# Low parts of every fourth weight chunk made on GpSimd instead of VectorE

## The chip, the cores and the metric

The kernel runs on one core of one Trainium2 chip. The metric is the device time of one execution in microseconds. TensorE (PE) multiplies, VectorE (DVE) and ScalarE (ACT) work elementwise, SyncE (SP) issues the loads of the weights, and GpSimd (POOL) does nothing after four constants at the start.

## The reference, cut to what matters

Two blocks run one after the other on 256 tokens of 2048 features. The first has a retention layer (8 heads) and a sliding-window attention layer (16 query heads, 4 key and value heads); both have an adaptive norm before them. The second has three parallel branches (block attention, dilated attention, attention over a memory) that gates merge. In skeleton:

```
h   = rms_norm(x) * (1 + scale) + shift        # scale, shift: cond @ ada_w
p   = h @ w_in                                 # queries, keys, values, gates
y   = mixer(p) * silu(gate)
x   = x + gt * (y @ w_out)                     # twice, then the second block
```

Everything is float32, and nearly all the time goes into `h @ w`, with weights of some 490 MB that pass through the core once. To reach float32 accuracy with faster products, each weight matrix and each activation is split into a rounded high part and a low part, and three products are summed: high by high, low by high, high by low.

## The kernel before

**The stream.** All weights are laid out on the host as 936 chunks of 128 partitions by 1024 floats (512 KB), in the order of use. SP issues one load after another into four raw slots (eight in the beginning) (`sync_program`, L479). 192 of the chunks (`ada_w`, for the conditioning) go to TensorE as they are (L559). The other 744, the split chunks, numbered n = 0 to 743 in this text, go through three engines:

- ScalarE copies raw to `w_hi[n % 4]`, which rounds it (L932). It waits for the load and for the products of split chunk n - 4, which used the slot before.
- VectorE subtracts: `w_lo[n % 4] = raw - w_hi[n % 4]` (L1413). It waits for `s.hi >= n + 1` and counts `s.lo` up.
- TensorE waits for `s.lo` (L501) and runs the products of the chunk: 24 matmuls for most (L506 to L508), three for each 128 by 128 block.

The raw slot is free again when `w_lo` of its chunk is made: SP waits there for `s.lo` (L478), or for TensorE's count where the slot held an unsplit chunk.

**The order.** Each engine has its own program, written by hand; nothing is reordered on the chip. On ScalarE and VectorE the splitting is mixed in among the other work: `weights_to(c)`, called before nearly every step, splits all chunks up to three beyond chunk c. So `w_lo` stands in line behind whatever VectorE does, and what follows on VectorE stands behind `w_lo`, also while VectorE waits for ScalarE's high part.

**The attention stage** (four groups `kv`, L1794 to L1841, 2000 to 2410 us) is the part in which VectorE has the most to do for each chunk. A head's `softmax` (L1744) adds the mask (L1752), takes the maximum (L1758), lets ScalarE make the exponentials (L1169) and scales (L1771). Behind it stand two `w_lo`, then a gate or a copy (L1481, L1724), then the softmax of the next head. `norm` (L1726) and `rotate` (L1468) serve the queries of the next group: reciprocal (L1729), scaling (L1731), two products and a sum (L1472, L1473, L1475), with ScalarE's swap between them (L1003, L1004).

**Names in the rows.** `a_s` are the scores of a head, `a_q` the queries, `a_rstd` their norm (`nrstd` in the code), `a_g` the gate, `o_lo` and `h_lo` low parts of activations. L1546 and L1550 make normed activations of the memory and their low parts at the start. `b_s` are the scores of the second block.

Of the kernel before, what the change touches and what calls it, by code (L numbers as in the profile page):

```python
# [6 lines left out]
F32, F32R, BF16 = mybir.dt.float32, mybir.dt.float32r, mybir.dt.bfloat16  # L7
# [32 lines left out]
SLOTS = 4  # L40
# [206 lines left out]
for _c in range(CHUNKS):  # L247
    _n = BEFORE[_c] + 1 if BEFORE[_c] is not None and RAW_USE[BEFORE[_c]] else 0
    NEEDS.append(max(_n, NEEDS[-1] if NEEDS else 0))

GROUPS = [what[1:] for what in WHERE if what[0] == "ada"]

# [67 lines left out]
class Signals:  # L320
    def __init__(self, nc, ctx, known):
        def sem(name):
            return ctx.enter_context(nc.semaphore(f"s_{name}"))
        self.hi, self.lo, self.mm = sem("hi"), sem("lo"), sem("mm")
        self.raw = [sem(f"raw{i}") for i in range(WIDE)]
        self.load = {name: sem(f"load_{name}") for name in LOADS}
        self.banks = Banks([sem(f"emptied{b}") for b in range(BANKS)], known.get("banks", {}))
        self.by_name = {name: Signal(sem(name), known.get(name, {})) for name in SIGNALS}

    def __getitem__(self, name):  # L330
        return self.by_name[name]

    def found(self):
# [136 lines left out]
def sync_program(nc, m, s, d):  # L470
    sp = nc.sync
    sp.dma_start(m.par[:, :], d["params"]).then_inc(s.load["par"], 16)
    for c in range(CHUNKS):
        slot, before = SLOT[c], BEFORE[c]
        if before is not None and RAW_USE[before]:
            sp.wait_ge(s.mm, before + 1)
        elif before is not None:
            sp.wait_ge(s.lo, Q[before] + 1)  # L478
        sp.dma_start(m.raw[slot][:, :], d["stream"][c]).then_inc(s.raw[slot], 16)  # L479
# [9 lines left out]
def tensor_program(nc, m, s):  # L489
# [10 lines left out]
    def weights(c):  # L500
        pe.wait_ge(s.lo, Q[c] + 1)  # L501
        return m.w_hi[Q[c] % SLOTS], m.w_lo[Q[c] % SLOTS]
# [897 lines left out]
def vector_program(nc, m, s):  # L1400
# [5 lines left out]
    def weights_to(c):  # L1406

        while split[0] < min(Q[c] + SLOTS, len(SPLIT)) and NEEDS[SPLIT[split[0]]] <= c:
            n, raw = split[0], SPLIT[split[0]]
            split[0] += 1  # L1410
            dve.wait_ge(s.hi, n + 1)
            slot = n % SLOTS
            dve.tensor_tensor(m.w_lo[slot][:, :], m.raw[SLOT[raw]][:, :], m.w_hi[slot][:, :].bitcast(F32), ALU.subtract  # L1413
                              ).then_inc(s.lo, 1)

# [540 lines left out]


def build(nc, d, known):
    with ExitStack() as ctx:
# [4 lines left out]
        scalar_program(nc, m, s, d)  # L1964
        vector_program(nc, m, s)
        return s.found()

# [44 lines left out]
```

## Time and profile before

| | us |
|---|---|
| median of 3 runs | 3493.75 (3493.48 to 3502.49) |
| profiled execution, own time | 3492.97 |
| its span, first to last instruction | 3491.7 |
| TensorE busy | 3264.7 (93%) |
| VectorE busy | 1738.8 (50%), of it `w_lo` 901.5 |
| ScalarE busy | 1260.3 (36%), of it `w_hi` 779.1 |
| GpSimd busy | 0.2 |

TensorE's share of busy time is a mean. It is 100% between 3020 and 3380 us and 99% in the long retention stage (450 to 1800 us), and 86% in the attention stage. The chain of waits, which follows the last instruction back to what released it, spends 85% of the span on TensorE, 6% on VectorE, 3% each on ScalarE and on loads. So a microsecond on VectorE counts where the chain passes through VectorE, and nowhere else.

### The profile page before, as it was taken

What the parts mean: (1) busy time and instruction counts of PE and PEld (TensorE: products, weight loads), DVE (VectorE), ACT (ScalarE), POOL (GpSimd) and SP (SyncE); (2) the same over time, 40 slices, a digit from 0 to 9 for tenths busy, and PEclk for the clock granted to TensorE, in tenths of its full rate; (3) what the DMA queues carried; (4) which work ended last, traced back from release to release, by engine and by line L of the source; (5) the groups of instructions that cost most, each with busy time, mean ns of one, the idle gap of its engine ahead of it and who ended that gap; (6) DMA issues with size and microseconds to landing.
All of it is one profiled execution on the core that took longest, in us unless ns stands there. A gap on an engine that the chain in (4) does not pass through costs nothing.

```text
span 3491.7 us, 47726 instructions
## 1 busy us (share of the span) xinstructions
PE 3264.7 (93%) x20298; PEld 2782.5 (80%) x20298; DVE 1738.8 (50%) x2491; ACT 1260.3 (36%) x1779; POOL 0.2 (0%) x4
## 2 busy tenths in 40 slices
PE   5979999999999999999997988987999999999998
PEld 3757677777777777777866878876999998999998
DVE  4533243434334343433436667766666555555555
ACT  3432222222222222222224454444554444444443
POOL 0000000000000000000000000000000000000000
PEclk9989999999999999999998999998999999999999
DMA  7753433333332333323243324443545444466654
GB/s 302 285 186 145 171 117 116 105 127 121 109 129 101 109 103 127 127 103 133 97 144 122 115 97 133 133 133 115 172 148 167 151 150 165 151 196 194 195 188 151
DMA packets 141635, 508.93 MB, mean 146 GB/s; under 512 B 15344, under 2 KB 19568, under 8 KB 140656
## 3 DMA queue, kind: packets, MB, share of 16 engines
q1 hardware_dynamic: 137040, 493.03, 41.5%
q10 hardware_dynamic: 4384, 12.85, 1.0%
q8 instruction: 161, 2.64, 0.3%
q14 instruction: 50, 0.41, 0.0%
HBM read 501.62 MB, written 4.19 MB: 145 GB/s over the span
## 4 chain that ended last, share of the span: by engine, by line
PE 85%; DVE 6%; DMA 3%; ACT 3%; issue 2%; SPq 0%; ACTq 0%; DVEq 0%
PE bank L506 26%; PE bank L508 25%; PE bank L507 25%; DMA raw<-stream 3%; PE bank L559 2%; PE bank L672 2%; DVE w_lo L1413 1%; PE bank L757 1%; PE bank L738 1%; PE bank L658 1%; PE bank L674 1%; DVE a_rstd L1729 1%; ACT a_s L1169 1%; PE bank L748 0%; ACT w_hi L932 0%
## 5 line engine op out<-in xcount | busy, mean ns | idle before, releaser
L506 PE MATMUL bank<-h_hi,w_hi 128*128 128x256 f32 (+1 forms) x4032 | 1269.0, 315 | 23.9 <-DVE w_lo L1413 21.6
L1413 DVE TENSOR_TENSOR w_lo<-raw,w_hi 128x1024 fp32r<-128x1024 f32 x744 | 901.5, 1223 | 695.5 <-ACT w_hi L932 690.6
L507 PE MATMUL bank<-h_lo,w_hi 128*128 128x256 f32 (+1 forms) x4032 | 1244.7, 309 | 0.0
L508 PE MATMUL bank<-h_hi,w_lo 128*128 128x256 f32 (+1 forms) x4032 | 1244.7, 309 | 0.0
L932 ACT ACTIVATE w_hi<-raw 128x1024 fp32r<-128x1024 f32 x744 | 779.1, 1057 | 1059.5 <-PE bank L508 601.5
L506 PEld LDWEIGHTS bank<-h_hi,w_hi 128*128 128x128 f32 x4032 | 762.5, 189 | 92.5 <-issue 36.8
L507 PEld LDWEIGHTS bank<-h_lo,w_hi 128*128 128x128 f32 x4032 | 763.4, 189 | 46.6 <-issue 4.9
L508 PEld LDWEIGHTS bank<-h_hi,w_lo 128*128 128x128 f32 x4032 | 761.2, 189 | 43.6
L506 PE MATMUL bank<-w_hi,h_hi 128*128 128x512 f32 x704 | 288.4, 410 | 44.9 <-DVE w_lo L1413 40.6
L508 PE MATMUL bank<-w_hi,h_lo 128*128 128x512 f32 x704 | 279.5, 397 | 0.0
L507 PE MATMUL bank<-w_lo,h_hi 128*128 128x512 f32 x704 | 279.0, 396 | 0.0
L1603 DVE SCALAR_TENSOR_TENSOR res<-bank,mod,res 128x256 f32<-128x256 f32 x320 | 134.1, 478 | 167.9 <-PE bank L508 167.9
L506 PE MATMUL bank<-o_hi,w_hi 128*128 128x512 f32 x512 | 201.6, 394 | 10.1 <-ACT vg L992 8.3
L506 PEld LDWEIGHTS bank<-w_hi,h_hi 128*128 128x128 f32 x704 | 135.1, 192 | 88.2 <-issue 51.8
L507 PE MATMUL bank<-o_lo,w_hi 128*128 128x512 f32 x512 | 200.5, 392 | 0.0
L508 PE MATMUL bank<-o_hi,w_lo 128*128 128x512 f32 x512 | 200.5, 392 | 0.0
L508 PEld LDWEIGHTS bank<-w_hi,h_lo 128*128 128x128 f32 x704 | 134.6, 191 | 29.6
L507 PEld LDWEIGHTS bank<-w_lo,h_hi 128*128 128x128 f32 x704 | 135.0, 192 | 29.0 <-issue 1.7
L559 PE MATMUL bank<-raw,cond 128*32 128x256 f32 x1536 | 119.6, 413 | 32.8 <-DMA raw<-stream 32.8
L506 PEld LDWEIGHTS bank<-o_hi,w_hi 128*128 128x128 f32 x512 | 97.0, 189 | 32.5 <-issue 12.5
L507 PEld LDWEIGHTS bank<-o_lo,w_hi 128*128 128x128 f32 x512 | 97.0, 190 | 20.0
L508 PEld LDWEIGHTS bank<-o_hi,w_lo 128*128 128x128 f32 x512 | 96.8, 189 | 20.3
(215 smaller groups left out, 2698.5 us busy)
## 6 DMA issues: line engine op xcount, KB each, us to landing
raw<-stream SPq DMA_DIRECT2D x936, 512.0 KB, 4.2
res<-tokens_in ACTq DMA_DIRECT2D x4, 1024.0 KB, 13.7
vg<-mem_in ACTq DMA_DIRECT2D x4, 512.0 KB, 10.7
res<-mem_kv ACTq DMA_DIRECT2D x2, 1024.0 KB, 10.0
out<-res SPq DMA_DIRECT2D x4, 512.0 KB, 3.0
mem_kv<-qk ACTq DMA_DIRECT2D x1, 1024.0 KB, 7.8
mem_kv<-vg ACTq DMA_DIRECT2D x1, 1024.0 KB, 11.1
tab<-tables ACTq DMA_DIRECT2D x1, 513.0 KB, 4.3
```

Of the source, the lines that this page charges most:

```text
L506: pe.matmul(out, sh, mh, start=start, stop=False)
L507: pe.matmul(out, sh, ml, start=False, stop=False)
L508: return pe.matmul(out, sl, mh, start=False, stop=stop)
L559: mm = pe.matmul(out[32 * j:32 * j + 32, 0:L], m.cond[:, 4 * c + j, :], m.raw[SLOT[chunk]][:, j * L:(j + 1) * L], start=c == 0, stop=c == 3)
L658: mm = pe.matmul(outs[mt][:, :], m.qk[:, 2 + dt, L + mt * P:L + (mt + 1) * P], m.qk[:, dt, :], start=dt == 0, stop=dt == 1)
L672: pe.matmul(out[:, :], m.v[:, 2 + mt, dv], m.s_ctx[:, mt, :], start=mt == 0, stop=mt == 1)
L674: mm = pe.matmul(out[:, LAT], m.v[:, mt, dv], m.s_lat[:, mt, :], start=False, stop=mt == 1, skip_group_check=True)
L738: mm = pe.matmul(out[:, at - a0:at - a0 + n], q[:, qs], k, start=i == 0, stop=i == len(pairs) - 1)
L757: mm = pe.matmul(out[:, LAT], v, pt[:, kt, :], start=kt == 0, stop=kt == len(tiles) - 1)
L932: act.activation(m.w_hi[n % SLOTS][:, :], m.raw[SLOT[raw]][:, :], ACT.Copy).then_inc(s.hi, 1)
L1413: dve.tensor_tensor(m.w_lo[slot][:, :], m.raw[SLOT[raw]][:, :], m.w_hi[slot][:, :].bitcast(F32), ALU.subtract).then_inc(s.lo, 1)
L1603: i = dve.scalar_tensor_tensor(out=m.res[:, tile, cols], in0=psum(*what)[:, cols], scalar=m.mod[layer][:, 2 * KT + tile, side:side + 1], i ...
```

## The change

Every split chunk with n % 4 = 3 has its low part made by GpSimd, in a program of its own that contains nothing else. VectorE makes the other three of four. The slot `w_lo[3]` and `w_hi[3]` then belongs to GpSimd's chunks alone. Each of the two engines has its own semaphore, and `lo(n)` gives for a chunk the semaphore and the count to wait for; TensorE and SP wait for that one.

```diff
+BY_POOL = [n % SLOTS == SLOTS - 1 for n in range(len(SPLIT))]
+LOW = [n // SLOTS + 1 if BY_POOL[n] else n - n // SLOTS + 1 for n in range(len(SPLIT))]
...
-        self.hi, self.lo, self.mm = sem("hi"), sem("lo"), sem("mm")
+        self.hi, self.mm = sem("hi"), sem("mm")
+        self.lo_dve, self.lo_pool = sem("lo_dve"), sem("lo_pool")
...
+    def lo(self, n):
+
+        return (self.lo_pool, LOW[n]) if BY_POOL[n] else (self.lo_dve, LOW[n])
...
-            sp.wait_ge(s.lo, Q[before] + 1)
+            sp.wait_ge(*s.lo(Q[before]))
...
-        pe.wait_ge(s.lo, Q[c] + 1)
+        pe.wait_ge(*s.lo(Q[c]))
...
+            if BY_POOL[n]:
+                continue
             dve.wait_ge(s.hi, n + 1)
             slot = n % SLOTS
             dve.tensor_tensor(m.w_lo[slot][:, :], m.raw[SLOT[raw]][:, :], m.w_hi[slot][:, :].bitcast(F32), ALU.subtract
-                              ).then_inc(s.lo, 1)
+                              ).then_inc(s.lo_dve, 1)
...
+def pool_program(nc, m, s):
+    pool = nc.gpsimd
+    for n, raw in enumerate(SPLIT):
+        if BY_POOL[n]:
+            slot = n % SLOTS
+            pool.wait_ge(s.hi, n + 1)
+            pool.tensor_tensor(m.w_lo[slot][:, :], m.raw[SLOT[raw]][:, :], m.w_hi[slot][:, :].bitcast(F32), ALU.subtract
+                               ).then_inc(s.lo_pool, 1)
```

Lines of the changed kernel stand 8 to 10 lower than before in the parts named here: L1413 becomes L1423, L1771 becomes L1781, L1475 becomes L1485. GpSimd's instruction is L1977.

VectorE, before, at the end of the first softmax of an attention group (the kernel's 2044 to 2048 us); `w_lo3` is the low part of a chunk with n % 4 = 3:

```order
L1768 RECIPROCAL a_numbers0_89<-a_numbers0_89 128x2
L1771 TENSOR_SCALAR a_s0_87<-a_s0_87,a_numbers0_89 128x512 x2
L1413 TENSOR_TENSOR w_lo3<-raw3,w_hi3 128x1024
L1413 TENSOR_TENSOR w_lo0<-raw0,w_hi0 128x1024
L1481 SCALAR_TENSOR_TENSOR a_g_83<-a_g_83,bank6 128x256
L1752 TENSOR_TENSOR a_s1_88<-bank7,a_mask_92 128x512
```

VectorE in the changed kernel, at the same place:

```order
L1778 RECIPROCAL a_numbers0_89<-a_numbers0_89 128x2
L1781 TENSOR_SCALAR a_s0_87<-a_s0_87,a_numbers0_89 128x512 x2
L1423 TENSOR_TENSOR w_lo0<-raw0,w_hi0 128x1024
L1491 SCALAR_TENSOR_TENSOR a_g_83<-a_g_83,bank6 128x256
L1762 TENSOR_TENSOR a_s1_88<-bank7,a_mask_92 128x512
```

The first of the two subtractions has gone from VectorE's line, the second moved up behind the scaling.

VectorE, before, where the queries of the next group are rotated (2086 to 2091 us):

```order
L1472 TENSOR_TENSOR a_q_75<-a_q_75,a_rope_91 128x512
L1473 TENSOR_TENSOR a_rstd0_81<-a_rstd0_81,a_rope_91 128x512
L1475 TENSOR_TENSOR a_q_75<-a_q_75,a_rstd0_81 128x512
L1413 TENSOR_TENSOR w_lo3<-raw3,w_hi3 128x1024
L1413 TENSOR_TENSOR w_lo0<-raw0,w_hi0 128x1024
L1724 COPY a_q_75<-bank1 128x256
```

VectorE in the changed kernel, at the same place:

```order
L1482 TENSOR_TENSOR a_q_75<-a_q_75,a_rope_91 128x512
L1483 TENSOR_TENSOR a_rstd0_81<-a_rstd0_81,a_rope_91 128x512
L1485 TENSOR_TENSOR a_q_75<-a_q_75,a_rstd0_81 128x512
L1423 TENSOR_TENSOR w_lo0<-raw0,w_hi0 128x1024
L1734 COPY a_q_75<-bank1 128x256
```

Here `w_lo3` stood behind the whole rotation; on GpSimd it stands behind nothing.

GpSimd in the changed kernel, from its start (before, it had the constants alone):

```order
L2026 MEMSET const-float32-1.0 128x1
L2026 MEMSET const-bfloat16-1.0 128x1
L2026 MEMSET const-uint8-127 128x1
L1977 ISA
L1977 TENSOR_TENSOR w_lo3<-raw3,w_hi3 128x1024 x7
L1977 TENSOR_TENSOR w_lo3<-raw7_74,w_hi3 128x1024 x3
L1977 TENSOR_TENSOR w_lo3<-raw1,w_hi3 128x1024 x6
```

The list goes on like this to 186 subtractions, with no other work among them.

## Rows read from the trace of the kernel before

**Rows 1.** The page: busy time of each engine, and the chain by engine.
```profile
PE 3264.7 (93%) x20298; PEld 2782.5 (80%) x20298; DVE 1738.8 (50%) x2491; ACT 1260.3 (36%) x1779; POOL 0.2 (0%) x4
...
PE 85%; DVE 6%; DMA 3%; ACT 3%; issue 2%; SPq 0%; ACTq 0%; DVEq 0%
```

**Rows 2.** Busy time by stretch: stretch, length, then each engine (instructions), clock, DMA.
```profile
450.00:1800.00 1350.00, 1341.68 (x6158) 1040.59 (x6157) 526.88 (x762) 347.36 (x449) 0.00 (x0) 1.00 0.32 114
...
2000.00:2410.00 410.00, 352.83 (x2508) 318.11 (x2506) 282.84 (x427) 193.27 (x317) 0.00 (x0) 0.95 0.37 119
...
3020.00:3380.00 360.00, 360.00 (x3179) 360.00 (x3179) 204.31 (x240) 159.15 (x194) 0.00 (x0) 1.00 0.61 193
```

**Rows 3.** Groups by line: count, busy us, mean ns, idle time before.
```profile
L1413 DVE TENSOR_TENSOR w_lo<-raw,w_hi 128x1024 fp32r<-128x1024 f32 x744 | 901.5, 1223 | 695.5 <-ACT w_hi L932 690.6
L932 ACT ACTIVATE w_hi<-raw 128x1024 fp32r<-128x1024 f32 x744 | 779.1, 1057 | 1059.5 <-PE bank L508 601.5
```

**Rows 4.** Slowest elementwise form on VectorE, from the groups by form.
```profile
L1729 DVE RECIPROCAL a_rstd<-a_rstd 128x512 f32<-128x512 f32 x12 | 40.2, 3352 | 19.4 <-ACT a_rstd L970 19.4
```

**Rows 5.** TensorE's waits in the attention stage, 2000 to 2410 us.
```profile
PE bank L506 <- DVE w_lo L1413: 18.4, 7, 8.0
```

**Rows 6.** The chain over the whole span: first and last of seven such pieces.
```profile
2045.19 2.27 DVE w_lo L1413 x2
...
2341.38 2.27 DVE w_lo L1413 x2
```

**Rows 7.** Timeline of ScalarE and VectorE, 2043.7 to 2049.1 us: start, length.
```profile
2043.78 1.99 ACT L932 ACTIVATE w_hi<-raw 128x1024 fp32r<-128x1024 f32 x2
...
2044.31 0.88 DVE L1771 TENSOR_SCALAR a_s<-a_s,a_numbers 128x512 f32<-128x512 f32 x2
2045.10 2.35 DVE L1413 TENSOR_TENSOR w_lo<-raw,w_hi 128x1024 fp32r<-128x1024 f32 x2
...
2049.09 1.22 DVE L1758 TENSOR_REDUCE a_numbers<-a_s 128x2 f32<-128x1024 f32 x1
```

**Rows 8.** Timeline of ScalarE and VectorE, 2086.4 to 2091.2 us, at the rotation.
```profile
2086.43 2.01 ACT L932 ACTIVATE w_hi<-raw 128x1024 fp32r<-128x1024 f32 x2
...
2087.12 0.68 DVE L1473 TENSOR_TENSOR a_rstd<-a_rstd,a_rope 128x512 f32<-128x512 f32 x1
2087.84 0.69 DVE L1475 TENSOR_TENSOR a_q<-a_q,a_rstd 128x512 f32<-128x512 f32 x1
2088.45 2.35 DVE L1413 TENSOR_TENSOR w_lo<-raw,w_hi 128x1024 fp32r<-128x1024 f32 x2
```

**Rows 9.** The same, 2106 to 2109.5 us, and the chain there.
```profile
2106.04 3.90 ACT L932 ACTIVATE w_hi<-raw 128x1024 fp32r<-128x1024 f32 x4
...
2106.73 0.69 DVE L1473 TENSOR_TENSOR a_rstd<-a_rstd,a_rope 128x512 f32<-128x512 f32 x1
...
2108.14 1.15 DVE w_lo L1413
...
2109.42 0.55 PE bank L506
```

**Rows 10.** Timeline of ScalarE and VectorE, 2030 to 2034.5 us, before the first softmax.
```profile
2030.25 2.00 ACT L932 ACTIVATE w_hi<-raw 128x1024 fp32r<-128x1024 f32 x2 [0.78 <-DVE a_sinks L1798]
...
2031.41 2.36 DVE L1413 TENSOR_TENSOR w_lo<-raw,w_hi 128x1024 fp32r<-128x1024 f32 x2 [1.19 <-ACT w_hi L932]
```

**Rows 11.** Timeline, 52.9 to 62 us, at the start: one high part, then VectorE.
```profile
53.07 1.04 ACT L932 ACTIVATE w_hi<-raw 128x1024 fp32r<-128x1024 f32 x1
...
54.09 1.67 DVE L1546 SCALAR_TENSOR_TENSOR s_ctx<-vg,par,rstd 128x256 f32<-128x256 f32 x4
...
60.19 2.36 DVE L1413 TENSOR_TENSOR w_lo<-raw,w_hi 128x1024 fp32r<-128x1024 f32 x2
```

**Rows 12.** Timeline, 395 to 400 us, in the first retention head.
```profile
395.46 1.04 ACT L932 ACTIVATE w_hi<-raw 128x1024 fp32r<-128x1024 f32 x1
...
397.22 1.22 DVE L1413 TENSOR_TENSOR w_lo<-raw,w_hi 128x1024 fp32r<-128x1024 f32 x1
```

More of the change, by code:

```diff
@@ L1965, in build @@
         vector_program(nc, m, s)
+        pool_program(nc, m, s)
         return s.found()
```

## The prediction, made before the changed kernel was run

> **What bounds the kernel now.** The page comes first: TensorE is busy for 93% of the span and carries 85% of the chain, VectorE 6%, some 210 us [rows 1]. The table of stretches then says where VectorE can matter. From 450 to 1800 us TensorE is busy for 1341.7 of 1350 us and from 3020 to 3380 us for all of 360, with VectorE at 39% and 57% [rows 2]: there VectorE can become some microseconds later or earlier and nothing ends later. From 2000 to 2410 us TensorE is busy for 352.8 of 410 us and VectorE for 282.8 [rows 2], and TensorE waits 18.4 us for low parts [rows 5]. This stage decides. One kind of piece returns in its chain, two `w_lo` in a row for 2.27 us, seven times [rows 6]: two in each of the first three groups, one in the last. Counting the subtractions of the whole timeline up to there, the first of each pair is a chunk with n % 4 = 3.
>
> **What the change moves.** It takes 186 of the 744 subtractions, 186 x 1.223 us = 227 us [rows 3], from VectorE and gives them to GpSimd. That sum says nothing of the span, since most of it lies under TensorE. Three things do: how long one takes on GpSimd, when it can start, and what VectorE does meanwhile.
>
> **How long.** No row shows GpSimd at arithmetic. VectorE takes 1.22 us for 1024 elements from two operands [rows 3] and also 1.22 us for 1024 from one, the maximum [rows 7]; ScalarE needs 1.06 us for one operand [rows 3]. So 1.22 us is the lower end, an engine as good as VectorE. The upper end is the slowest form on VectorE, the reciprocal: 3352 ns for 512 elements [rows 4], so 6.7 us for 1024. Between the two I take an engine that reads its operands one after the other at about ScalarE's or VectorE's speed: 2 x 1.06 to 2 x 1.22, so 2.1 to 2.4; I take 2.3 us, near the lower end because the copy and the subtraction, not the reciprocal, are the rows of this kind of work. The Trainium skill has a measured pair for this (GPSIMD Engine Reference, Elementwise — side-by-side cycle accounting): 4497 ns against VectorE's 2293 ns for 2048 elements, by which an estimate for 1024 would be 2.25 us; the trace agrees with VectorE's half of it (1.223 us) and cannot show the other.
>
> **Who waits for whom.** VectorE reads two operands in the time of one [rows 3, 7], and its scaling of scores, one operand, passes 512 elements in 0.44 us (0.88 for two) [rows 7] where a two-operand product of 512 takes 0.69 [rows 8]. So VectorE has a second way into the memory, used for the second operand or to double the rate of one. GpSimd needs a way in too. The ends for what its 2.3 us cost VectorE are zero (a way of its own) and the whole of it (it holds VectorE's second way, and a two-operand instruction of VectorE waits). I take the whole as the likelier: VectorE's second way is the only spare one that the rows hint at. No row shows the two side by side, so this is a judgement, and the zero end is the first rival. The Trainium skill has a rule that speaks against this change (SBUF — State Buffer, Who interferes with whom): a two-input VectorE instruction and a GpSimd one that reads SBUF exclude each other, and whichever comes second waits for the whole of the other. By it the sum is the one below, without it the first rival's; no row of before can test it.
>
> **The sum, place by place,** with 2.3 us for the instruction and VectorE held meanwhile:
>
> 1. *Behind the softmax, seven times.* Today the scaling ends at 2045.19, both subtractions at 2047.46 [rows 6, 7]. The first high part is ready at about 2044.83 (1.06 us after 2043.78) [rows 7, 3], so GpSimd asks while VectorE still scales, and gets its turn at 2045.19. It ends at 2047.49; VectorE's own subtraction then runs to 2048.71. That is 1.25 later each, 8.8 in all. The next head's scores stand behind it.
> 2. *At the rotation, three times.* The high part is ready at 2087.50, while VectorE is in L1473 (to 2087.80) [rows 8]. GpSimd runs 2087.8 to 2090.1, then L1475 (0.69) and one subtraction (1.22) end at about 2091.95; today both subtractions are done at 2090.80 [rows 8]. Some 1.15 each, 3.5 in all.
> 3. *Before the output product, three times.* The high part is ready at about 2107.10, GpSimd runs from 2107.42 to 2109.7, and TensorE, which started at 2109.42 behind a `w_lo` that ended at 2109.29 [rows 9], starts at 2109.85: 0.43 each, 1.3 in all.
> 4. *Before the first softmax, once.* TensorE waits for this low part alone, 8.0 us, the longest of its seven waits [rows 5]. High part at 2031.31, `w_lo` 2031.41 plus 1.22 today [rows 10], plus 2.3 then: 1.1.
> 5. *At the start, once.* Chunk 3 is rounded by 54.11; VectorE runs two-operand instructions back to back until chunk 0's `w_lo` at 60.19, for which TensorE waits [rows 11]. If GpSimd comes between them: 2.3.
> 6. *In the first retention head, two chunks with n % 4 = 3.* At one the high part is ready at 396.50 and `w_lo` ends at 398.44 today [rows 12]; behind VectorE's instruction of the moment GpSimd ends at about 398.95: 0.5. At the other VectorE starts at once today, so 1.08 is lost, of which 0.3 is slack: 0.8. Together 1.3.
>
> Sum: 8.8 + 3.5 + 1.3 + 1.1 + 2.3 + 1.3 = 18.3 us. On the profiled execution's 3492.97 us (span 3491.7 and 1.3 around it) that is 3511.3; the median of the runs, 3493.75, is 0.8 above it, so the forecast is **3512 us**, 0.5% slower.
>
> **What I cost at nothing.** The second semaphore: the number of waits of TensorE and SP stays the same. Loads behind GpSimd's chunks: SP waits there for a low part that comes 1.1 us later, and all later loads stand behind this wait; but in the stretches with TensorE at 99 to 100% a chunk's 24 products take at least 2.7 us (360 us by 3179 products is 0.113 us each [rows 2]), the ring holds four, and no load is in the chain. Without that cover it would be 1.1 us for each fourth chunk, 200 us at most. VectorE held in the retention stage: up to 2.3 us for each fourth chunk, under a VectorE that is idle for 61% of the time [rows 2]. The relief of VectorE: real only where the chain passes through it, and taken in above.
>
> **Rivals.**
>
> *GpSimd disturbs nobody.* Then its chunk is made beside VectorE's. Behind the softmax VectorE's own subtraction waits only for the second high part (ready 2045.77) and ends at 2047.09, 0.37 earlier, times seven 2.6. At the rotation it starts 1.1 earlier, times three 3.3. Against it stand 0.15 times three in place 3, 1.1 in place 4 and 1.3 in place 6. Result -3.0: 3491 us, within what a measurement tells from nothing. For it: ScalarE and VectorE work side by side throughout and `w_lo` still takes 1223 ns on the mean [rows 3]. Chance 0.36. This is also the case in which VectorE's relief shows; for more than 10 us faster GpSimd would have to be as quick as VectorE and more places free than the chain shows.
>
> *VectorE goes first and GpSimd waits.* Then place 1 gains as above (-2.6), but at the rotation GpSimd starts behind L1475 and VectorE's next subtraction, at 2089.75, and ends at 2092.05 where `w_lo` was done at 2089.67: 2.4 each, 7.1. Place 3 costs 1.15 each, 3.5, place 4 1.1 and place 6 2.0. Sum +11: 3505 us. Chance 0.16. It decides as soon as VectorE's instructions are granted before a waiting GpSimd.
>
> *The instruction is long.* With 3.3 us instead of 2.3 each of the 17 places costs 1 us more, 3529 us; with 6.7 us, 75 us more, 3587 us. Chance 0.08 for over 3.3.
>
> The forecast's own case has 0.40. Its time is the likeliest single one; it and the two behind it lie on the slow side.
>
> **How the numbers follow.** A measurement of this kernel can tell about 0.3% (10.5 us) from no change, so slower begins at 3504. Of the forecast's case I put three quarters beyond it (0.30), since places 1 and 2 can come out smaller; of the second rival 0.09, all of the long instruction 0.08, and 0.01 of the first: slower 0.48. Faster 0.04, out of the first rival. The rest, 0.48, is within. The range runs from 3486, below the first rival, to 3529, the instruction at 3.3 us with VectorE held; the long case's 0.08 and a part of the tails stay outside.
>
> **What the new profile would show.** GpSimd with 186 subtractions, 2.3 us from start to start where two follow closely. If the forecast is right, VectorE's `w_lo`, L1475 or `h_lo` beside them are longer or later than 1.22 and 0.69 us, the seven pieces of 2.27 us become about 3.5 us from the end of the scaling to the end of the one subtraction, and the attention stage is 15 us longer. If VectorE's rows keep their durations and the pieces shrink to 1.9 us, it is the first rival. Retention and the stretch from 3020 us must stay as long as they are; if not, the loads behind GpSimd's chunks are what I left out.

## The result: 1% slower, 3532 us

| | before | changed |
|---|---|---|
| median of the runs, us | 3493.6 (4 runs, 3492.6 to 3502.5) | 3532.3 (4 runs, 3525.5 to 3532.9) |
| ratio | | 1.0097, 95% interval 1.0077 to 1.0117 |
| profiled execution, us | 3492.97 (span 3491.7) | 3532.8 (span 3531.3) |

The sign is the one forecast (3512), the size is not: +39 us instead of +18, and the median lies 3 us above the top of the range. In the changed kernel lines stand 8 to 10 later: L506 is L514, L932 is L940, L1413 is L1423, L1475 is L1485, L1870 is L1880; GpSimd's subtraction is L1977.

The page of the changed kernel, busy time and chain by engine, answers to [rows 1]:

```profile
PE 3285.5 (93%) x20298; PEld 2800.1 (79%) x20298; DVE 1618.0 (46%) x2305; ACT 1259.9 (36%) x1779; POOL 456.9 (13%) x190
...
PE 83%; DVE 7%; ACT 4%; DMA 3%; issue 2%; POOL 0%; SPq 0%; ACTq 0%; DVEq 0%
```

VectorE has 121 us less work (1738.8 less 1618.0), not the 227 us of the subtractions it gave away, and still its share of the chain rose from 6% to 7%. The groups say where the other 106 us are (count, busy us, mean ns, idle before), against [rows 3]:

```profile
L1423 DVE TENSOR_TENSOR w_lo<-raw,w_hi 128x1024 fp32r<-128x1024 f32 x558 | 747.1, 1345 | 642.8 <-ACT w_hi L940 638.8
...
L1977 POOL TENSOR_TENSOR w_lo<-raw,w_hi 128x1024 fp32r<-128x1024 f32 x186 | 456.7, 2455 | 3053.3 <-ACT w_hi L940 3053.3
```

GpSimd's instruction takes 2.46 us on the mean and 2.40 where nothing disturbs it (forecast 2.3). VectorE's own low parts went from 1223 to 1345 ns, though their form is the same: 558 times 0.122 are 68 of the 106 us, and most of the rest is in its other two-operand instructions. The busy times by stretch, to be read against [rows 2]:

```profile
450.00:1800.00 1350.00, 1341.71 (x6165) 1041.74 (x6163) 475.17 (x713) 347.15 (x448) 128.88 (x53) 1.00 0.32 114
2000.00:2430.00 430.00, 364.34 (x2538) 327.03 (x2536) 290.35 (x409) 196.71 (x322) 56.96 (x23) 0.93 0.35 115
3050.00:3400.00 350.00, 348.58 (x3068) 348.05 (x3067) 163.19 (x204) 154.96 (x189) 76.80 (x32) 1.00 0.57 190
```

In these stretches of retention TensorE's busy time is what it was (1341.71 us, before 1341.68), and from 3050 us it still has work all the time, as forecast; what retention lost nonetheless is in the table below. In the attention stage the granted clock fell from 0.95 to 0.93.

**Where the time went.** I took from both traces when TensorE starts the first product of each of the 744 pieces (the split chunks, by their number n); the difference grows like this (us):

| pieces | stage | forecast | changed | changed, again (below) |
|---|---|---|---|---|
| 0 to 64 | start, first retention head | 3.6 | 4.1 | 5.8 |
| 64 to 288 | retention | 0 | 3.1 | 1.3 |
| 288 to 312 | before attention | 0 | -0.2 | 0.6 |
| 312 to 396 | attention | 14.7 | 13.0 | 15.7 |
| 396 to 416 | | 0 | -0.1 | 0.8 |
| 416 to 468 | block-sparse heads | 0 | 13.4 | 14.9 |
| 468 to 712 | dilated, memory, merge | 0 | 1.5 | 3.2 |
| 712 to end | last product | 0 | 4.9 | 0.0 |
| sum | | 18.3 | 39.7 | 42.3 |

The stages that the sum names came out as summed, 17.1 us against 18.3. More than half of the loss lies where the sum had nothing.

The pages split it in another way. TensorE has the same 20298 products, but its busy time grew by 20.8 us (3285.5 less 3264.7) and its idle time by 18.8 (245.8 against 227.0 of the two spans): by the profile, which models the ends of products, half of the loss is longer waits, the other half is products that take longer.

**Behind the softmax** (place 1 of the sum). Timeline of VectorE and GpSimd, to be read beside [rows 7]:

```profile
2051.65 0.88 DVE L1781 TENSOR_SCALAR a_s<-a_s,a_numbers 128x512 f32<-128x512 f32 x2
2053.14 2.68 DVE L1423 TENSOR_TENSOR w_lo<-raw,w_hi 128x1024 fp32r<-128x1024 f32 x1 [0.61 <-ACT w_hi L940]
...
2052.25 2.50 POOL L1977 TENSOR_TENSOR w_lo<-raw,w_hi 128x1024 fp32r<-128x1024 f32 x1 [11.49 <-ACT w_hi L940]
```

GpSimd runs to 2054.75. VectorE's subtraction is issued at 2053.14, lasts 2.68 us instead of 1.22 and ends 1.1 us after GpSimd's: it stood still for as long as GpSimd ran. GpSimd did not wait for the end of the scaling, as the prediction had it: it starts 0.28 us before that, and takes 2.50 us instead of 2.40. From the end of the scaling to the end of the second low part it is now 3.30 us where it was 2.27 [rows 6, 7].

**At the rotation** (place 2), against [rows 8]:

```profile
2098.58 2.77 DVE L1485 TENSOR_TENSOR a_q<-a_q,a_rstd 128x512 f32<-128x512 f32 x1
2101.28 1.22 DVE L1423 TENSOR_TENSOR w_lo<-raw,w_hi 128x1024 fp32r<-128x1024 f32 x1
...
2098.31 2.49 POOL L1977 TENSOR_TENSOR w_lo<-raw,w_hi 128x1024 fp32r<-128x1024 f32 x1 [22.89 <-ACT w_hi L940]
```

The rotation's product of 512 elements lasts 2.77 us instead of 0.69. It is not the low part alone that is held, but whichever two-operand instruction VectorE has next.

**In the block-sparse heads** the sum had nothing. Before: the timeline of VectorE and of ScalarE (L1176), then the chain at the same head (the last two lines).

```profile
2498.99 0.62 DVE L1771 TENSOR_SCALAR b_s<-b_s,b_numbers 128x256 f32<-128x256 f32 x2
2499.74 2.36 DVE L1413 TENSOR_TENSOR w_lo<-raw,w_hi 128x1024 fp32r<-128x1024 f32 x2
2502.01 0.42 DVE L1870 TENSOR_SCALAR res<-bank 128x256 f32<-128x256 f32 x1
...
2506.89 0.42 DVE L1870 TENSOR_SCALAR res<-bank 128x256 f32<-128x256 f32 x1
...
2508.22 0.60 ACT L1176 ACTIVATE res<-bank 128x512 f32<-128x512 f32 x1
...
2507.29 1.62 issue
...
2510.01 0.12 PE bank L506
```

The same head in the changed kernel, with GpSimd's line between them:

```profile
2520.25 0.61 DVE L1781 TENSOR_SCALAR b_s<-b_s,b_numbers 128x256 f32<-128x256 f32 x2
2521.95 2.58 DVE L1423 TENSOR_TENSOR w_lo<-raw,w_hi 128x1024 fp32r<-128x1024 f32 x1 [1.08 <-ACT w_hi L940]
2524.45 0.41 DVE L1880 TENSOR_SCALAR res<-bank 128x256 f32<-128x256 f32 x1
...
2529.31 0.42 DVE L1880 TENSOR_SCALAR res<-bank 128x256 f32<-128x256 f32 x1
...
2530.62 0.60 ACT L1184 ACTIVATE res<-bank 128x512 f32<-128x512 f32 x1
...
2521.05 2.40 POOL L1977 TENSOR_TENSOR w_lo<-raw,w_hi 128x1024 fp32r<-128x1024 f32 x1 [14.26 <-ACT w_hi L940]
...
2528.56 2.76 issue
...
2532.76 0.21 PE bank L514
```

L1880 copies the next head's keys, then its queries, out of their banks. The first copy starts 3.6 us after the scaling instead of 2.4 (2524.45 less 2520.86; 2502.01 less 2499.61), and the second, 4.9 us behind the first in both kernels, is as much later. ScalarE waits for each of them with its half swaps, and behind the swaps of the queries stands its copy of the turned probabilities of the head before (L1176, now L1184). For this copy TensorE waits, between the turning (L748) and the product of the probabilities with the values (L757): 2.76 us instead of 1.62. TensorE's waits of the whole stage, before and changed (total, times, longest):

```profile
PE bank L757 <- issue: 11.3, 7, 1.6
```

```profile
PE bank L765 <- issue: 19.3, 7, 3.0
```

Then comes the second part: behind the longer wait TensorE's products take 0.21 us each, where before they went on at 0.12. The granted clock of the stage (last but two column) says the same, first before, then changed:

```profile
2459.00:2631.00 172.00, 160.66 (x1339) 157.65 (x1338) 114.91 (x196) 89.77 (x149) 0.00 (x0) 1.00 0.50 160
...
2479.00:2664.00 185.00, 165.70 (x1335) 162.50 (x1334) 113.49 (x183) 89.06 (x149) 31.27 (x13) 0.96 0.43 146
```

Over the whole trace TensorE was granted 1.2 GHz in 22 stretches of 158.7 us together before, and in 30 stretches of 199.0 us in the changed kernel. At half speed 40 us more are up to 20 us lost, up to half of the whole difference; 13.7 of those 40 us are in the attention stage and 13.7 in the block-sparse heads, which had none.

### The profile page after: what moved, and what is told of

It reads as the page before. It is cut to its first block, busy times and chain, and to the rows that moved or that the text cites. A ratio compares the mean times of both kernels' runs of the same rounds, so it can differ in the third digit from the quotient of the medians.

```text
span 3531.3 us, 47728 instructions
## 1 busy us (share of the span) xinstructions
PE 3285.5 (93%) x20298; PEld 2800.1 (79%) x20298; DVE 1618.0 (46%) x2305; ACT 1259.9 (36%) x1779; POOL 456.9 (13%) x190
## 4 chain that ended last, share of the span: by engine, by line
PE 83%; DVE 7%; ACT 4%; DMA 3%; issue 2%; POOL 0%; SPq 0%; ACTq 0%; DVEq 0%
PE bank L514 25%; PE bank L516 24%; PE bank L515 24%; DMA raw<-stream 3%; PE bank L567 2%; PE bank L680 2%; DVE w_lo L1423 2%; ACT w_hi L940 1%; PE bank L765 1%; DVE a_rstd L1739 1%; PE bank L746 1%; PE bank L666 1%; PE bank L682 1%; ACT a_s L1177 1%; POOL w_lo L1977 0%
## 5 line engine op out<-in xcount | busy, mean ns | idle before, releaser
L514 PE MATMUL bank<-h_hi,w_hi 128*128 128x256 f32 (+1 forms) x4032 | 1275.7, 316 | 25.6 <-DVE w_lo L1423 13.4
L940 ACT ACTIVATE w_hi<-raw 128x1024 fp32r<-128x1024 f32 x744 | 778.8, 1057 | 1061.7 <-PE bank L516 611.8
L1423 DVE TENSOR_TENSOR w_lo<-raw,w_hi 128x1024 fp32r<-128x1024 f32 x558 | 747.1, 1345 | 642.8 <-ACT w_hi L940 638.8
L1977 POOL TENSOR_TENSOR w_lo<-raw,w_hi 128x1024 fp32r<-128x1024 f32 x186 | 456.7, 2455 | 3053.3 <-ACT w_hi L940 3053.3
L514 PEld LDWEIGHTS bank<-h_hi,w_hi 128*128 128x128 f32 x4032 | 767.2, 190 | 94.7 <-issue 38.8
L514 PE MATMUL bank<-w_hi,h_hi 128*128 128x512 f32 x704 | 289.1, 411 | 46.1 <-DVE w_lo L1423 36.6
L514 PE MATMUL bank<-o_hi,w_hi 128*128 128x512 f32 x512 | 201.9, 394 | 10.9 <-ACT vg L1000 8.3
L514 PEld LDWEIGHTS bank<-w_hi,h_hi 128*128 128x128 f32 x704 | 135.3, 192 | 89.5 <-issue 52.6
L514 PEld LDWEIGHTS bank<-o_hi,w_hi 128*128 128x128 f32 x512 | 97.2, 190 | 33.3 <-issue 13.3
```

The lines of the kernel that those rows point to most:

```text
L514: pe.matmul(out, sh, mh, start=start, stop=False)
L940: act.activation(m.w_hi[n % SLOTS][:, :], m.raw[SLOT[raw]][:, :], ACT.Copy).then_inc(s.hi, 1)
L1977: pool.tensor_tensor(m.w_lo[slot][:, :], m.raw[SLOT[raw]][:, :], m.w_hi[slot][:, :].bitcast(F32), ALU.subtract).then_inc(s.lo_pool, 1)
```

## The experiments

Theory after the traces: (A) a GpSimd subtraction holds VectorE's two-operand instructions for its whole length; where VectorE's next instruction is on TensorE's path TensorE waits longer, and part of the longer waits brings the half clock with it. Rivals: (B) the loss comes from GpSimd's own low part being ready 1.2 us late; (C) it is a clock effect of the program as a whole. And, apart from the cause of the loss, a question: is it GpSimd that is wrong here, or the choice of pieces?

All kernels of this section but the idle ones are the changed kernel with another `BY_POOL`, and `LOW` counting whatever that gives:

```
-BY_POOL = [n % SLOTS == SLOTS - 1 for n in range(len(SPLIT))]
-LOW = [n // SLOTS + 1 if BY_POOL[n] else n - n // SLOTS + 1 for n in range(len(SPLIT))]
+BY_POOL = [<condition> for n in range(len(SPLIT))]
+LOW = [sum(BY_POOL[i] == BY_POOL[n] for i in range(n + 1)) for n in range(len(SPLIT))]
```

| run | pieces on GpSimd | median, us | before, same chip | ratio, 95% |
|---|---|---|---|---|
| e1 | attention, n % 4 = 3 | 3510.9 | 3499.5 | 1.0032 (1.0007 to 1.0056) |
| e2 | block heads, n % 4 = 3 | 3511.4 | 3499.5 | 1.0034 (1.0011 to 1.0056) |
| e3 | none; 34 idle subtractions | 3547.3 | 3499.5 | 1.0129 (1.0087 to 1.0170) |
| e4 | all even | 3466.1 | 3499.5 | 0.9896 (0.9859 to 0.9934) |
| e5 | n % 4 = 0 | 3476.1 | 3501.0 | 0.9915 (0.9885 to 0.9946) |
| e6 | 0, 32, 34, 36, 288 | 3474.8 | 3501.0 | 0.9905 (0.9874 to 0.9935) |
| e7 | retention and merge, n % 4 = 3 | 3496.3 | 3501.0 | 0.9982 (0.9962 to 1.0001) |
| e8 | 0, 32, 34, 36, even from 288 to 466 | 3447.3 | 3501.0 | 0.9832 (0.9801 to 0.9863) |
| e9 | none; 34 idle copies | 3523.1 | 3496.2 | 1.0074 (1.0053 to 1.0095) |
| e10 | none; 34 idle fills | 3498.6 | 3496.2 | 0.9997 (0.9979 to 1.0015) |
| e11 | the change once more | 3538.2 | 3496.2 | 1.0104 (1.0071 to 1.0137) |
| e12 | 0, 1, 32 to 36, even from 288 to 394 | 3445.5 | 3496.2 | 0.9853 (0.9817 to 0.9888) |

The kernel before spread over 20 to 25 us on these chips, and the intervals reach 0.2 to 0.4% to each side; what a single stage costs is read from the traces, by the starts of the pieces as above.

### The two stages apart

e1, e2 and e7, in this order:

```
+BY_POOL = [n % SLOTS == SLOTS - 1 and 312 <= n < 396 for n in range(len(SPLIT))]
+BY_POOL = [n % SLOTS == SLOTS - 1 and 416 <= n < 468 for n in range(len(SPLIT))]
+BY_POOL = [n % SLOTS == SLOTS - 1 and (64 <= n < 280 or 584 <= n < 712) for n in range(len(SPLIT))]
```

> GpSimd makes every fourth low part only among pieces 312 to 395 (the attention stage, 21 subtractions); VectorE makes all others. Theory A, VectorE is held for the whole of each GpSimd subtraction and TensorE waits for the piece behind it: the stage is 12 to 15 us longer, as the trace of the changed kernel shows between these pieces (20.0 less 7.2 us), and the kernel takes 3505 to 3509 us. Rival B, the loss of the changed kernel is one of TensorE's clock over the whole program and not of these places: under 4 us, 3494 to 3498 us.

> GpSimd makes every fourth low part only among pieces 416 to 467 (the block-sparse stage, 13 subtractions). Theory A, the stage of itself costs what the trace of the changed kernel shows there (33.3 less 20.0 us), by the same holding of VectorE and by the lower granted clock behind the longer waits: 3505 to 3508 us. Rival B, these 13 us are a consequence of what went before (TensorE arrives in another clock state): under 4 us, 3494 to 3498 us. The prediction had put this stage at nothing: 3493 to 3495 us.

> GpSimd makes every fourth low part among pieces 64 to 279 (retention) and 584 to 711 (the merge), 86 subtractions; VectorE makes the others. The prediction put both stages at nothing since TensorE has work queued there; by the traces of before and after they cost 2.6 and 0 us. Theory A: 0 to 4 us above before (ratio 1.000 to 1.001). Rival B, the missing 20 us of the sum lie in many small delays in the covered stretches: 8 us or more (ratio above 1.002).

*e1:* TensorE's starts shift by 0.3 us up to piece 312 and by 11.0 at piece 396, so the stage costs 10.7 us (13.0 in the full change), a little under the 12 to 15 expected; 10.2 us more of the stage were at half clock (1.2 GHz). *e2:* 1.8 us at piece 416, 15.9 at 468: 14.1 us for the 13 subtractions, 13.7 us more at half clock. The block-sparse stage makes its loss of itself; that the attention stage comes first has no part in it, and rival (C) falls. The two together, 24.8 us, answer to the 26.4 us of the changed kernel. By the medians e1 and e2 are 11.4 and 11.9 us above before. *e7:* 86 subtractions moved TensorE by 0.1 us in retention and by nothing in the merge, and the ratio includes 1. The cover that the prediction named holds.

### Who is held, and by what

GpSimd gets work that nobody waits for, in the kernel before, at 34 places that are those of the changed kernel in the two stages:

```
+    for n, raw in enumerate(SPLIT):
+        if n % SLOTS == SLOTS - 1 and (312 <= n < 396 or 416 <= n < 468):
...
+            pool.wait_ge(s.hi, n + 1)
+            pool.tensor_tensor(m.tab[:, 0:896], m.tab[:, 0:896], m.tab[:, 0:896], ALU.subtract).then_inc(s.ghost, 1)
```

That is e3; e9 and e10 have in place of the last line

```
+            pool.tensor_copy(m.tab[:, 0:896], m.tab[:, 0:896]).then_inc(s.ghost, 1)
+            pool.memset(m.tab[:, 0:896], 0.0).then_inc(s.ghost, 1)
```

> The kernel before, VectorE makes every low part; GpSimd beside it makes 34 subtractions of 896 columns from a table that is no longer used, each started by the same high part as in the changed kernel, and nobody waits for their results. Theory A, the cost is VectorE being held: VectorE's low parts beside them last 1.8 to 2.2 us, and the time is 15 to 28 us above before, 3508 to 3521 us. Rival B, the cost is that GpSimd's own low part comes 1.2 us later than VectorE's would: then nothing waits for these, 3493 to 3496 us.

> As the kernel with idle subtractions, but each of GpSimd's 34 idle instructions copies the 896 columns onto themselves: one input read instead of two. Theory A, VectorE is kept out whenever GpSimd reads at all: VectorE's low parts beside them last well over 1.22 us in proportion to the copy's own time, and the kernel is 15 to 45 us above before. Rival B, only a GpSimd instruction with two inputs keeps VectorE out: VectorE's low parts stay at 1.22 us and the kernel within 3 us of before (ratio 0.999 to 1.001).

> As the kernel with idle subtractions, but each of GpSimd's 34 idle instructions only writes zeros to the 896 columns: no input is read. Theory A, it is GpSimd's reading that keeps VectorE's two-input instructions out: low parts beside the fills last 1.22 us and the kernel is within 3 us of before (ratio 0.999 to 1.001). Rival B, any GpSimd instruction on the memory holds them: they last as long as the fill, and the kernel is above ratio 1.003.

The groups in the stretch from 2459 to 2660 us, VectorE's low parts and GpSimd's idle instruction, in this order for the subtraction, the copy and the fill:

```profile
L1414 DVE TENSOR_TENSOR w_lo<-raw,w_hi 128x1024 fp32r<-128x1024 f32 x56 | 80.1, 1452 | 33.7 <-ACT w_hi L933 32.7
L1968 POOL TENSOR_TENSOR tab<-tab 128x896 f32<-128x896 f32 x12 | 32.4, 2699 | 215.1 <-ACT w_hi L933 215.1
...
L1414 DVE TENSOR_TENSOR w_lo<-raw,w_hi 128x1024 fp32r<-128x1024 f32 x59 | 77.5, 1335 | 29.4 <-ACT w_hi L933 28.2
L1968 POOL COPY tab<-tab 128x896 f32<-128x896 f32 x13 | 21.2, 1628 | 234.3 <-ACT w_hi L933 234.3
...
L1414 DVE TENSOR_TENSOR w_lo<-raw,w_hi 128x1024 fp32r<-128x1024 f32 x61 | 73.3, 1223 | 20.5 <-ACT w_hi L933 19.2
L1968 POOL MEMSET tab<- 128x896 f32 x13 | 11.1, 850 | 236.4 <-ACT w_hi L933 236.4
```

Over both stages, one instruction at a time (means, us):

| idle instruction | undisturbed | started 0.24 before the end of a scaling (L1772) | started inside a low part of VectorE | a low part of VectorE started inside it | loss from piece 312 to 468 |
|---|---|---|---|---|---|
| subtraction, 2 inputs | 1.68 (one only) | 1.76 | 2.67 | 2.34 | 45.0 |
| copy, 1 input | 0.94 | 1.03 | 1.95 | 1.82 | 21.6 |
| fill, no input | 0.85 | 1.03 | 0.85 | 1.22 | -1.0 |

The hold goes both ways: a copy that starts inside VectorE's 1.22 us takes 1.95, a low part that starts inside a copy ends 1.07 us after it. The expectation for e9 named as theory A that any reading counts, and that is what came; two inputs are not needed on GpSimd's side. A fill and a low part do not hold each other. (Six of each kind started 0.19 us before the end of a two-operand product, L1474; they took 1.71, 0.98 and 0.85 us.) VectorE's scaling with one operand is another matter: all seven fills that started beside one took 1.03 us, all others 0.85 to 0.86. One of the seven, VectorE and then GpSimd in e10:

```profile
2045.91 0.88 DVE L1772 TENSOR_SCALAR a_s<-a_s,a_numbers 128x512 f32<-128x512 f32 x2
...
2046.55 1.03 POOL L1968 MEMSET tab<- 128x896 f32 x1 [13.33 <-ACT w_hi L933]
```

That costs GpSimd 0.2 us at most and VectorE nothing. e3 was put at 15 to 28 us and cost 48 by the medians. Its low parts were held longer than the 1.8 to 2.2 us expected (2.34 on the mean, up to 2.71), and the expectation left out the clock again: the trace of e3 has 30.7 us more at half clock in the attention stage and 20.5 in the block-sparse heads than the kernel before. Nobody waits for these results, so rival (B) is not needed for the loss; it has its share at place 4 below, where TensorE waits for GpSimd's own low part and loses 1.1 us. An idle subtraction costs more than the real one, since VectorE still makes its own low part besides.

The Trainium skill (SBUF — State Buffer, Who interferes with whom) states this rule: a VectorE instruction with two SBUF inputs contends with a GpSimd one that reads SBUF, not with one that only writes. All three runs agree, with the numbers of the table.

### The same number of subtractions, other pieces

In the changed kernel the piece that goes to GpSimd is the first of each pair behind the softmax, and VectorE makes the second, which must wait. What if it is the second?

In this order e4, e5, e6, e8 and e12:

```
+BY_POOL = [n % 2 == 0 for n in range(len(SPLIT))]
+BY_POOL = [n % SLOTS == 0 for n in range(len(SPLIT))]
+BY_POOL = [n in (0, 32, 34, 36, 288) for n in range(len(SPLIT))]
+BY_POOL = [n in (0, 32, 34, 36) or (n % 2 == 0 and 288 <= n < 468) for n in range(len(SPLIT))]
+BY_POOL = [n in (0, 1, 32, 33, 34, 35, 36) or (n % 2 == 0 and 288 <= n < 396) for n in range(len(SPLIT))]
```

> As many subtractions on GpSimd as in the changed kernel (186), but of pieces 0, 4, 8 and so on instead of 3, 7, 11 and so on; VectorE makes the rest. Theory A, what counts is which piece of a pair goes: TensorE now waits first for piece 3, 7, 11, whose low part VectorE starts at once and alone, GpSimd's stands behind it, and pieces 0, 32, 36 and 288 no longer queue behind VectorE's own work: 20 to 35 us below before (ratio 0.990 to 0.994). Rival B, what counts is how many GpSimd subtractions hold VectorE: as the changed kernel, 35 to 40 us above before (ratio 1.010 to 1.012).

> GpSimd makes the low part of every second piece (0, 2, 4 and so on, 372 of them), VectorE that of the others. Theory A, only what gates TensorE counts: the pieces 0, 32, 34, 36 and 288, for which TensorE waits 3.6 to 18.5 us behind VectorE's other work, are now GpSimd's and come earlier, and behind the softmax the two low parts of a pair run on two engines but exclude each other: between 20 us faster and 10 us slower than before, 3474 to 3504 us. Rival B, each GpSimd subtraction costs VectorE its 2.4 us wherever it stands, and there are twice as many of them: 3550 to 3590 us.

> GpSimd makes five low parts alone, of pieces 0, 32, 34, 36 and 288, each the first or nearly the first of a stage, for which TensorE waits while the low part is queued 5 to 15 us behind VectorE's other work in the kernel before. Theory A, the queue is what TensorE waits for there: 14 to 20 us below before (ratio 0.994 to 0.996). Rival B, TensorE's gap there is set by the normalised states that VectorE makes in the same time, and each GpSimd subtraction delays them: within 3 us of before (ratio 0.999 to 1.001).

*e5* has 186 GpSimd subtractions like the change and is 0.85% faster than before, where the change is 1% slower: the same instruction, the same number, another residue. By the trace TensorE is 31.7 us ahead of the kernel before at piece 468. Not all of it is the choice within a pair: 21.6 us are there by piece 288, most of them from pieces at the start for which TensorE used to wait (17.4 us by piece 64). What the choice within a pair does is read from the stages: in the attention stage e5 gains 12.7 us where the change lost 13.0, in the block-sparse heads it gains 0.4 where the change lost 13.4. *e4*, with 372 subtractions, is 38.6 us ahead at piece 468; its 3466 us lie 8 us below the range that was expected. The rival of both runs, a price for each subtraction, falls in both.

Where the gain at the start comes from is seen in *e6*, with five subtractions. TensorE's waits of the kernel before from 40 to 260 us (total, times, longest), then three of e6's:

```profile
PE bank L506 <- DVE w_lo L1413: 37.3, 4, 18.5
```

```profile
PE bank L514 <- DVE w_lo L1423: 6.6, 2, 3.8
...
PE bank L514 <- POOL w_lo L1977: 4.8, 1, 4.8
...
PE bank L514 <- issue: 3.9, 1, 3.9
```

And the longest of them, piece 32: ScalarE and VectorE of the kernel before, and GpSimd of e6.

```profile
172.62 1.06 ACT L932 ACTIVATE w_hi<-raw 128x1024 fp32r<-128x1024 f32 x1 [2.41 <-DMA raw<-stream]
...
186.40 1.29 DVE L1465 TENSOR_TENSOR h_lo<-decay,h_hi 128x512 fp32r<-128x512 f32 x2 [16.36 <-ACT h_hi L984]
...
188.81 2.35 DVE L1413 TENSOR_TENSOR w_lo<-raw,w_hi 128x1024 fp32r<-128x1024 f32 x2
```

```profile
171.38 2.34 POOL L1977 TENSOR_TENSOR w_lo<-raw,w_hi 128x1024 fp32r<-128x1024 f32 x1 [122.50 <-ACT w_hi L940]
```

The high part is ready at 173.68. VectorE is idle from 170.04 to 186.40, since the next instruction in its order waits for a high part of the states, and the low part stands behind that one: it starts at 188.81, and TensorE waits 18.5 us for it. VectorE has time, but not at this place of its order. GpSimd has an order of its own, and there the low part starts 0.1 us behind its high part. This gave 19.5 us up to piece 64 (expected 14 to 20) and 24.9 at piece 288 with the fifth. Of the fifth's 5.9 us most went again: at piece 312 the lead is 20.8. By the medians e6 is 26 us below before, more than the 14 to 20 expected; its trace ends 14.4 us ahead.

> GpSimd makes the low parts of pieces 0, 32, 34 and 36, and of every second piece from 288 to 466 (the even ones); VectorE makes the others. From the trace of the run with every even piece: 14 us saved by the four at the start, 6 us by piece 288, 22 us in the attention stage, nothing in the block stage. Theory A, these add up: 35 to 42 us below before (ratio 0.988 to 0.990). Rival B, part of the saving is given back in the later stages by TensorE running at 117.8 instead of 113.3 ns a product, as it did from 3050 us on in the run with every even piece: 20 to 27 us below (ratio 0.992 to 0.994).

> GpSimd makes the low parts of pieces 0, 1 and 32 to 36, and of the even ones from 288 to 394; VectorE makes the others, all of the block stage among them. Against the kernel with the chosen pieces this gives back the block stage's even pieces, which there moved the pieces by 0.4 us, and adds pieces 1, 33 and 35, for which TensorE still waits 2.0, 0 and 3.6 us. Theory A: 2 to 6 us below that kernel (3441 to 3446 us, ratio to before 0.981 to 0.983). Rival B, GpSimd makes pieces 33 and 35 later than VectorE would, since 2.4 us each stand behind each other, and holds VectorE's state products: 0 to 5 us above it.

*e8* is the best kernel that came of it, with *e12* level to it: 3447 and 3446 us, 1.5 to 1.7% below before and 2.4% below the change. In the trace of e8 TensorE is 28.3 us ahead at piece 288, 49.6 at 396, 50.0 at 468, and 46.0 at the end; 35 to 42 had been expected, so the gain is above both ranges. All of it is waiting: TensorE is busy for 3265.3 us where it was 3264.7 before, and idle for 180.3 of the span instead of 227.0. Its page, and its timeline behind a softmax (VectorE, then GpSimd), to be read against [rows 7] and against the changed kernel's above:

```profile
PE 3265.3 (95%) x20298; PEld 2782.9 (81%) x20298; DVE 1664.0 (48%) x2397; ACT 1261.5 (37%) x1779; POOL 241.4 (7%) x98
```

```profile
2016.88 0.88 DVE L1781 TENSOR_SCALAR a_s<-a_s,a_numbers 128x512 f32<-128x512 f32 x2
2017.68 1.22 DVE L1423 TENSOR_TENSOR w_lo<-raw,w_hi 128x1024 fp32r<-128x1024 f32 x1
2018.82 0.41 DVE L1491 SCALAR_TENSOR_TENSOR a_g<-a_g,bank 128x256 f32<-128x256 f32 x1
2019.15 1.28 DVE L1762 TENSOR_TENSOR a_s<-bank,a_mask 128x512 f32<-128x512 f32 x2
2020.53 1.22 DVE L1768 TENSOR_REDUCE a_numbers<-a_s 128x2 f32<-128x1024 f32 x1
```

```profile
2018.42 2.71 POOL L1977 TENSOR_TENSOR w_lo<-raw,w_hi 128x1024 fp32r<-128x1024 f32 x1 [6.92 <-ACT w_hi L940]
```

The scaling ends at 2017.76. VectorE's own low part comes first, and VectorE is through with it at 2018.90, 1.14 us behind the scaling instead of 2.27 before and 3.30 in the change. GpSimd's waits its turn (2.71 us), TensorE does not need it yet, and what VectorE has next (a product into `a_g` and the next scores, each with one operand in a bank, then a maximum) runs beside it at its usual 0.41, 1.28 and 1.22 us. The hold has not gone; it falls on work that has time. In the block-sparse stage the even pieces gained nothing: e8 has -49.6 before it and -50.0 behind it, and e12, without them there, -50.9 and -50.5. Of e12's two theories neither is shown: the additional pieces at the start brought 1.8 us up to piece 64 (23.2 ahead against 21.4), within what the times don't tell.

### The change again

> The changed kernel once more, on the same chip as the next two. It asks whether the stretch from 3440 us to the end, where TensorE ran at 117.8 ns a product instead of 113.3, and its cost of 5 us belong to the kernel. If to the kernel: the new trace has it at the same place and the time is 3525 to 3535 us again. If to the execution: the new trace has it elsewhere or not at all, its places between pieces 312 to 396 and 416 to 468 cost 12 to 14 us each again, and the times spread over 10 us or more.

The second trace of the changed kernel has the attention and block-sparse losses again (15.7 and 14.9 us, somewhat above the 12 to 14 expected) and 29 stretches at half clock of 199.8 us together. What it has not is the slow end: from 3450 to 3500 us, first the changed kernel, then its repetition (products of TensorE in brackets behind its busy time):

```profile
3450.00:3500.00 50.00, 50.00 (x427) 50.00 (x426) 23.88 (x30) 21.86 (x27) 12.00 (x5) 1.00 0.54 179
```

```profile
3450.00:3500.00 50.00, 50.00 (x443) 50.00 (x443) 26.40 (x33) 22.98 (x29) 9.60 (x4) 1.00 0.62 200
```

TensorE is never idle in either and the granted clock is 1.00 in both, and still a product starts each 117.8 ns in the one and each 113.3 ns in the other. So these 4.9 us belong to the execution and not to the kernel. The times of the repetition (3528.5 to 3550.8 in four runs) spread accordingly.

## Why the prediction was right in sign and 20 us short

The prediction had the mechanism and the sign; of the 39.7 us it had less than half.

- **The instruction's length:** 2.3 us forecast, 2.40 undisturbed, 2.46 on the mean. Right; 0.1 us at 17 places is under 2 us.
- **VectorE held for the whole:** right, and it decided between the forecast and the first rival. Rows 2053.14 and 2098.58 show it, e3, e9 and e10 by itself.
- **Place 1**, seven times: 1.03 us each (3.30 against 2.27), 7.2 in all; forecast 8.8. GpSimd starts 0.28 us before the scaling ends instead of behind it, and VectorE, once released, needs 1.07 us and not 1.22.
- **Place 2**, three times: from the high part's end to the second low part's end 4.26 us against 3.30, 0.96 each, 2.9 in all; forecast 3.5.
- **Place 3**, three times: TensorE's gap is 2.59, 2.47 and 2.82 us against 2.78, 2.77 and 2.47. Nothing on the mean; forecast 1.3.
- **Place 4:** 9.12 us against 8.02, the 1.1 forecast. **Place 5:** 2.1, forecast 2.3. **Place 6** and what else is up to piece 64: 2.0, forecast 1.3, with 4.5 us more at half clock in it.
- **The rivals:** VectorE goes first is excluded by the same rows, the long instruction by its 2.40 us.

Two steps failed, and both are omissions.

*The list of places ended with the attention stage.* I looked for TensorE's waits that name `w_lo` [rows 5] and for pieces of the chain that are `w_lo` [rows 6]. In the block-sparse heads the chain before has "issue" for 1.62 us in front of the product with the values, and no `w_lo`, although two low parts, 2.36 us together, stand right in front of L1870, from which that wait descends by way of ScalarE. An instruction that is queued ahead of the one that releases does not show as a releaser. Thirteen subtractions in that stage cost 13.4 us, of them 8 us in waits (TensorE's waits there called "issue" went from 11.3 to 19.3 us) and the rest, 5.4, is put down to the half clock (13.7 us of it, so up to 6.8 lost). e2 shows the stage's loss alone.

*The sum had no term for TensorE's clock.* It counted each lengthened wait at its length. In the changed kernel 40 us more ran at 1.2 GHz, up to 20 us lost; 27.3 of these 40 lie where waits grew, 13.7 us in each of the two stages. I had the clock of 0.95 in the attention stage before me [rows 2] and did not ask what longer waits would do to it. Two ways of adding up bound what it cost, and neither measures it alone. The places, one by one, are 15.3 us and 8.0 in the block-sparse stage; with 4.9 for the slow end that leaves 11.5 of the 39.7 us. But TensorE's idle time grew by 18.8 us only, so not all of the 23.3 reached it as waiting; of the 20.8 us by which its busy time grew, 4.9 are the slow end, and 15.9 are left. The bound of 20 is not reached by either.

Right was also what the prediction costed at nothing: loads, the semaphore, retention and the merge (e7). In the changed kernel itself retention lost 3.1 us, with 6.5 us more at half clock in it, and 1.3 in its second trace; since e7 has the same subtractions there up to piece 280 and loses nothing, this comes from what went before or from the execution, and which of the two is not shown.

What stays open: why TensorE, at full granted clock, is at 117.8 ns in some stretches and at 113.3 in others; and which lengthened wait brings half clock and which does not. In the same head 1.62 us did not and 2.76 us did, but no run varied one wait alone.

## What to carry to other kernels

Ask of work that moves to another engine what its operands' path holds up, and then who is next in line there: in the attention stage, giving away the first of a pair cost 13.0 us and giving away the second gained 12.7. An idle engine's own order can be worth more than its speed: five instructions that are twice as slow on GpSimd gained about 1%, since they no longer stood behind an instruction of VectorE that waited. Where a wait's releaser is named, look also at what is queued in front of that releaser on its engine, and where TensorE's waits grow, count its clock in.

## What the runs showed of the hardware

- A GpSimd instruction that reads and a VectorE instruction with two operands in SBUF exclude each other in both directions; whichever comes second stands still until the first has ended: copy 0.94 us undisturbed and 1.95 inside a low part; a low part 1.22 and 1.82 inside a copy. VectorE's instructions with one operand in a bank take 0.475 us beside GpSimd's subtractions and 0.477 elsewhere in the changed kernel, and a low part beside a fill takes its 1.22.
- VectorE's scaling of 512 elements, one operand in SBUF, 0.48 us, lengthens what GpSimd starts beside it, even a fill: 1.03 us against 0.85, copies 1.03 against 0.94, the real subtraction 2.50 against 2.40. Whether GpSimd holds such a scaling in turn the changed kernel does not show; there none starts inside a subtraction.
- GpSimd's subtraction takes 2.40 us for 1024 elements from two tiles; 896 elements of one tile subtracted from themselves take 1.68 us (once undisturbed), and a copy of them 0.94. Per element that is 2.3, 1.9 and 1.0 ns. The profile's spans on GpSimd are rough; here VectorE bears them out, since a held low part ends 1.07 to 1.08 us after GpSimd's end, with the copy and with the idle subtraction.
- The cadence of TensorE has two levels at the full granted clock, 113.3 and 117.8 ns for a product of 256 columns. A level held for up to 390 us, and the changes that were followed up lie at short stretches of half clock: in the changed kernel one of 3.4 us at 3426.2 us, with the slower level behind it to the end; in e4 one at 2971.6 (slower behind it) and one at 3367.5 (faster again); in e6 one at 3372.1 (slower). In e4 the slower level filled the stretch from 3050 us, with 2949 products where the changed kernel has 3068 in the same 350 us:

```profile
3050.00:3400.00 350.00, 347.70 (x2949) 347.50 (x2948) 123.05 (x164) 148.77 (x182) 147.11 (x62) 1.00 0.56 185
```

  That took 13.7 us of e4's lead (37.8 us at piece 584, 24.1 at 712), and 13.7 of e5's. GpSimd's work is not its cause: e6 has none there, and ran at 117.8 ns from 3370 us to its end. So the level of an execution alone moved the time by 4.9 us between the two traces of the changed kernel, and by 13.7 us in e4 and e5; a verdict on less needs the starts of the pieces, not the time.
